# A two-phase MLP in an encoder kernel: all up blocks by seven Strassen products, the whole down product as one Strassen step

## What is computed

```python
h = rmsnorm(x, norm_mix_pre);  z = h @ w_in
a = rmsnorm(mla(...));  r = hgrn2(...)            # attention and a linear recurrence
x = x + rmsnorm(concat([a, r]) @ w_o, norm_mix_post)
h = rmsnorm(x, norm_mlp_pre)
m = square(relu(h @ w_up)) @ w_down               # 1024 x 1024 x 4096, then 1024 x 4096 x 1024
x = x + rmsnorm(m, norm_mlp_post)
e = p @ w_ple;  gate = sigmoid(x @ w_ple_gate)
x = x + rmsnorm(e * gate, norm_ple)
```

## Time and profile before

| | before |
|---|---|
| median of three runs | 1456.87 us |
| profiled execution, first to last instruction | 1456.6 us |
| PE busy (7132 matmuls) | 1434.9 us, 99% |
| DVE busy | 827.7 us, 57% |
| POOL busy | 706.1 us, 48% |
| ACT busy | 562.9 us, 39% |
| DMA, mean over the span | 80 GB/s |

### The profile page before, as it was taken

How to read it: one execution, slowest core, us unless ns; L and a number is a source line. 1 busy time by engine, 2 the same in 40 slices (tenths; PEclk the granted TensorE clock), 3 DMA queues, 4 the chain that set the end, 5 groups by cost and what they waited for, 6 DMA issues and landing times.

```text
span 1456.6 us, 19156 instructions
## 1 busy us (share of the span) xinstructions
PE 1434.9 (99%) x7132; PEld 1196.1 (82%) x7132; DVE 827.7 (57%) x1110; ACT 562.9 (39%) x1057; POOL 706.1 (48%) x562
## 2 busy tenths in 40 slices
PE   6999999999999999999999999999999999999998
PEld 5888888878749998888888888888888888888886
DVE  7135555444688885258774865545545554446475
ACT  6223232234247665345324333332222323344452
POOL 4284636265206424456565654455544444454481
PEclk9999999999999999999999999999999999999999
DMA  5221111102240004433533311111111114623252
GB/s 202 66 66 36 30 37 29 26 23 58 66 101 2 1 1 139 156 107 127 204 100 96 92 58 52 58 46 56 44 44 58 52 58 145 201 89 117 87 160 93
DMA packets 91725, 115.94 MB, mean 80 GB/s; under 512 B 13681, under 2 KB 54641, under 8 KB 91121
## 3 DMA queue, kind: packets, MB, share of 16 engines
q1 hardware_dynamic: 91632, 114.72, 25.7%
HBM read 102.11 MB, written 10.49 MB: 77 GB/s over the span
## 4 chain that ended last, share of the span: by engine, by line
PE 92%; DVE 4%; issue 2%; POOL 1%; ACT 1%; DMA 0%; SPq 0%; DVEq 0%; POOLq 0%; ACTq 0%
PE ps L50 25%; PE ps L52 25%; PE ps L51 25%; PE ps L922 4%; PE ps L1630 3%; PE ps L1637 2%; PE ps L1015 1%; PE ps L1439 1%; PE ps L969 1%; PE ps L954 1%; PE ps L966 0%; DVE total L2058 0%; PE ps L1010 0%; PE ps L1012 0%; DMA lb_raw<-in_hg_lb 0%
## 5 line engine op out<-in xcount | busy, mean ns | idle before, releaser
L1352 POOL TENSOR_TENSOR wy_low<-w_raw,wy_high 128x512 fp32r<-128x512 f32 x230 | 331.5, 1442 | 361.8 <-ACT wy_high L1333 361.6
L1333 ACT ACTIVATE wy_high<-w_raw 128x512 fp32r<-128x512 f32 x230 | 145.1, 631 | 391.9 <-PE ps L52 386.2
L50 PE MATMUL ps<-wy_high,hid_high 128*128 128x512 f32 x512 | 199.3, 389 | 0.4 <-DVE hid_low L1962 0.4
L52 PE MATMUL ps<-wy_high,hid_low 128*128 128x512 f32 x512 | 199.2, 389 | 0.0
L51 PE MATMUL ps<-wy_low,hid_high 128*128 128x512 f32 x512 | 199.2, 389 | 0.0
L2048 DVE TENSOR_TENSOR total<-total,ps 128x512 f32<-128x512 f32 x184 | 124.8, 687 | 101.3 <-PE ps L52 101.3
L370 POOL TENSOR_TENSOR wx_low<-w_raw,wx_high 128x512 fp32r<-128x512 f32 (+1 forms) x64 | 84.8, 1331 | 142.4 <-ACT wx_high L472 142.4
L50 PE MATMUL ps<-a_high,wy_high 128*128 128x512 f32 x352 | 137.5, 391 | 0.0
L52 PE MATMUL ps<-a_high,wy_low 128*128 128x512 f32 x352 | 137.0, 389 | 0.0
L51 PE MATMUL ps<-a_low,wy_high 128*128 128x512 f32 x352 | 137.0, 389 | 0.0
L50 PEld LDWEIGHTS ps<-wy_high,hid_high 128*128 128x128 f32 x512 | 96.1, 188 | 20.6 <-issue 0.6
(11 more groups left out here) (246 smaller groups left out, 3038.1 us busy)
## 6 DMA issues: line engine op xcount, KB each, us to landing
w_raw<-in_w_up SPq DMA_DIRECT2D x88, 256.0 KB, 2.8
w_raw<-in_w_down SPq DMA_DIRECT2D x88, 256.0 KB, 2.6
w_raw<-in_w_in SPq DMA_DIRECT2D x62, 256.0 KB, 2.8
w_raw<-in_w_o SPq DMA_DIRECT2D x32, 256.0 KB, 2.7
w_raw<-in_w_ple_gate SPq DMA_DIRECT2D x32, 256.0 KB, 2.6
x_tile<-in_x SPq DMA_DIRECT2D x8, 512.0 KB, 7.1
x_res<-in_x SPq DMA_DIRECT2D x8, 512.0 KB, 5.9
keep_x<-x_res SPq DMA_DIRECT2D x8, 512.0 KB, 3.9
```

The lines of the kernel that those rows point to most:

```text
L50: pe.matmul(out, stat_high, mov_high, start=start, stop=False)
L52: return pe.matmul(out, stat_low, mov_high, start=False, stop=stop)
L1333: act.activation(out, tile_raw(tile), ACT.Copy).then_inc(high_made, 1)
L1352: pool.tensor_tensor(low_tile, tile_raw(tile), high_tile.bitcast(F32), ALU.subtract).then_inc(low_made, 1)
```

## The change

The MLP becomes two phases. In the first, all sixteen blocks of 256 hidden columns are Strassen blocks. Two of the seven products of each block (`ep`) come first for all blocks, 32 tiles, because they need the tokens of the first half alone; the other five (`st`) follow, block by block, 80 tiles. The hidden layer isn't split any more when it is made: it is kept as float32 in four quarters (`hid11`, `hid12`, `hid21`, `hid22`), 26 of 64 tiles of it in DRAM (`keep_h`). In the second phase the whole down product is one Strassen step of seven products (`m`), each of 16 tiles; for each tile the sum of two hidden tiles, the sum or difference of two weight tiles, and the high and low part of each are made just before PE uses them. A tile of `ep`, `st` and `m` is 12 matmuls. The weight ring has six slots where it had four. In a block, DVE now makes the differences t1 and t3, and POOL t2 (of t1) and t4 (of t2). Some semaphores of the front are merged.

The diff, cut:

```diff
-            st_order = ["b11", "t2", "b21", "t3", "t1", "t4", "b22"]
+            BLOCKS, PAIRED, EP_COLS = 16, 8, 2 * P
+            st_order = ["t2", "t3", "t1", "t4", "b22"]
+            products = ["m4", "m7", "m1", "m3", "m2", "m5", "m6"]
+            quads = {"m4": ("21", "11"), "m7": ("21", "22"), "m1": ("11", "22"), "m3": ("12", "22"), "m2": ("11",),
+                     "m5": ("22",), "m6": ("11", "12")}
...
+            segs += [("ep", f, 0, 0) for f in range(PAIRED)]
+            segs += [("st", b, 0, 0) for b in range(BLOCKS)]
+            segs += [("m", j, 0, 0) for j in range(7)]
...
+            depth = {"wo": 8, "ep": 4, "st": 5, "m": 16, "gate": 8, "e": 2, "gr": 0}
...
-            RING, AHEAD = 4, 2
+            RING, AHEAD, APAIRS = 6, 2, 3
...
+                      tiles_of[EP_TILE + 6]: [(1, 4)], tiles_of[EP_TILE + 10]: [(1, 5)],
+                      tiles_of[EP_TILE + 12]: [(1, 6)], tiles_of[EP_TILE + 14]: [(1, 7)],
+                      (M6, 8): [(2, 0)], (M6, 10): [(2, 1)], (M6, 12): [(2, 2)], (M6, 14): [(2, 3)],
...
+            def pool_sums(n):
...
+                if kind == "st":
+                    return st_order[k] in ("t2", "t4")
+                return kind == "m" and products[segs[tiles_of[n][0]][1]] in ("m7", "m1", "m6") and k % 2 == 1
...
             def low(pool, n):
                 if n < TILES:
+                    if pool_sums(n + 1):
+                        weight_sum(pool, n + 1)
                     low_part(pool, ("pair", n))
+                    if n in difference_after:
+                        hidden_difference(pool, difference_after[n])
...
+            def weight_sum(pool, n):
...
+                if st_order[k] == "t2":
+                    raw_ready(pool, ("b22", b))
+                    pool.wait_ge(t_made, 2 * b + 1)
+                    one, two = raw_tile(("b22", b)), t_sum[1][:, :]
...
+            def op_high_of(act, n):
...
+                if n - M_TILE >= APAIRS:
+                    act.wait_ge(done, done_at["tile", n - APAIRS])
...
             def high(act, n):
                 if n < TILES:
                     high_of(act, ("pair", n))
...
+                if in_m(n):
+                    op_high_of(act, n)
...
+                        if n - base in ((3, 5), (4, 7))[h]:
+                            two = slice(4 * h + (n - base) // 5 * 2, 4 * h + (n - base) // 5 * 2 + 2)
                             roots_of(mean7x_made, two.start // 2 + 1, mean7x, rstd7x, rstd7x_made, two)
...
+                def first_sum(b):
+                    dve.wait_ge(p1_made, b + 1)
+                    dve.wait_ge(done, done_at["tile", EP_TILE + 4 * (b // 2) + 2 + b % 2])
...
+                    dve.tensor_tensor(first_tile(b)[:, :], p1_kept[:, b, :], ps[:, 2 + b % 2, :],
+                                      ALU.add).then_inc(first_added, 1)
...
                     tile7(o)
                     tile7(o + 1)
+                    if h:
+                        first_sum(0)
+                        first_sum(1)
...
+                first_sum(6)
+                first_sum(7)
+                s_chain(s1_raw, [(1, a21[0]), (1, a22[0]), (1, a21[1]), (1, a22[1])])
+                dve.wait_ge(s_step, s_steps[0])
+                s_chain(s2_raw, [(1, s1_raw), (-1, a11[0]), (-1, a11[1])])
+                first_sum(8)
+                first_sum(9)
+                dve.wait_ge(x_moved, 2 * 16 * TT)
+                s_chain(s3_raw, [(1, a11[0]), (-1, a21[0]), (1, a11[1]), (-1, a21[1])])
+                first_sum(10)
+                first_sum(11)
+                s_chain(s4_raw, [(1, a12[0]), (-1, s2_raw), (1, a12[1])])
+                s_low_of(1, s1_raw, 0)
+                s_low_of(3, s3_raw, 2)
+                first_sum(12)
+                first_sum(13)
+                s_low_of(2, s2_raw, 4)
+                s_low_of(4, s4_raw, 6)
+                weight_sums(0)
+                first_sum(14)
+                first_sum(15)
+                for b in range(BLOCKS):
...
+                    dve.wait_ge(done, late_done(b, 2))
+                    dve.wait_ge(u_made, 3 * b + 2)
...
+                    dve.tensor_tensor(comb1[:, :], u3[:, :], ps[:, late_bank(b, 2), :], ALU.add).then_inc(comb_made, 1)
+                    dve.tensor_tensor(u2[:, :], u2[:, :], ps[:, late_bank(b, 2), :], ALU.add).then_inc(u_made, 1)
+                    if b < BLOCKS - 1:
+                        weight_sums(b + 1)
+                    else:
+                        down_weight_sum(M_TILE)
+                    dve.wait_ge(done, late_done(b, 3))
...
+                    if b == BLOCKS - 1:
+                        down_weight_sum(M_TILE + 1)
+                        operand_low(M_TILE)
...
+                for n in range(M_TILE, M_TILE + MSTEPS):
+                    down_weight_sum(n + 3)
+                    operand_sum(n + 3)
+                    operand_low(n + 2)
+                    name, k = m_step(n)
...
+                    if behind == "m5":
+                        if k < 4:
+                            add_out("m5", k, "11")
+                            add_out("m5", k, "12")
...
+                        if k in (8, 9):
+                            add8(k - 8)
+                        if k in (11, 13):
+                            add8(2 + (k - 11) // 2)
...
+                def first_product(s, k, wh, wl):
+                    b, rows = 2 * segs[s][1] + k % 2, k // 2
+                    if b < 2:
+                        pe.wait_ge(a_split, 16 + 8)
+                    elif rows:
+                        pe.wait_ge(first_added, b - 1)
```

More of the change, by code:

```diff
@@ L1069, in banks_of @@
                     return [4 * n + i for i in range(4)]
[L1070 to L1075 removed]
+                if kind == "ep":
+                    return [0]
                 if kind == "st":
                     return [0]
+                if kind == "m":
+                    return [4 * ((f + 1) % 2) + i for i in range(4)]
                 if kind == "gate":
@@ L1166, in back_of @@
                         done_at["turn", a, b, part] = count
-                elif kind == "mm" and segs[a][0] == "st":
-                    count += 1
-                    done_at["prod", a, b] = done_at["tile", first[a] + b] = count
                 elif kind == "mm":
@@ L1323, in high_of @@
                 else:
-                    s, k = tiles_of[tile[1]]
-                    act.wait_ge(low_made, place["sum", st_order[k], segs[s][1]] + 1)
+                    sum_ready(act, tile[1])
                 if tile[0] == "res":
@@ L1990, in s_chain @@
-                            dve.tensor_tensor(out[here], left[here], part[here],
+                            dve.tensor_tensor(out[here], left[here], taken[here],
                                               ALU.add if sign > 0 else ALU.subtract).then_inc(s_step, 1)
@@ new lines, in down_weight_sum @@
+                def down_weight_sum(n):
+                    if n not in w_sum_at:
+                        return
+                    name, k = m_step(n)
+                    one, two = (("w" + quad, n) for quad in quads[name])
+                    raw_ready(dve, one)
+                    raw_ready(dve, two)
+                    if n == M_TILE + 1:
+                        dve.wait_ge(late_made, 2 * (3 * (BLOCKS - 1) + 1))
+                    elif sum_before(n) is not None:
+                        dve.wait_ge(low_made, place["pair", sum_before(n)] + 1)
+                    dve.tensor_tensor(sum_tile(n), raw_tile(one), raw_tile(two),
+                                      ALU.subtract if name in minus else ALU.add).then_inc(w_sum_made, 1)
@@ L2165, in dve_tail @@
+                dve.wait_ge(gains9_in, 32)
+                for i in range(4):
+                    add_out("m6", i, "22")
                 means8(1)
@@ L2254, in bank_free @@
+                    elif kind == "m" and f >= 2:
+                        out_read(pe, products[f - 2], i)
+                    elif kind == "m":
+                        bank = banks_of(s)[i]
+                        late_read(pe, *max((b, k) for b in (BLOCKS - 2, BLOCKS - 1) for k in range(5) if late_bank(b, k) == bank))
                     elif s == G00:
-                        pe.wait_ge(summed, sum_at[D10, i])
+                        pe.wait_ge(a_split, 32 + (6 if i < 2 else 8))
                     elif s == G01:
```

975 lines of the change are left out of this document (480 added, 495 removed).

## The result

The kernel after the change takes 1512.84 us (median of four runs, 1511.91 to 1513.88), the kernel before 1456.57 us beside it (four runs): a ratio of 1.0386, 95% interval 1.0371 to 1.0401. It is 3.9% slower, where 1.3% was forecast; the time lies above the range of 1452 to 1500. The profiled execution spans 1510.2 us.

The account below looks back on a forecast made before the run. PE was taken to bound the kernel: 264 fewer matmuls save 59.8 us of 1456.6, giving 1396.8. Adding 37 + 18 + 1 + 8 + 15 - 0.8 gave 1475 us, 1.3% slower; range 1452 to 1500.

Parts of the forecast that it names:

- the four places: Late blocks, early tiles, down product and turns inside m6, where engines' lists would make PE wait: 37, 18, 9, 15 us.
- Place 1: Late blocks: POOL's t2, waiting for DVE's t1, delays the fifth tile's low part; 2.48 us a block, 37 us.
- Place 2: Early tiles: DVE's chains, low parts and first_sums don't keep up with PE; 18 us of waits.
- rival of a covered block chain: Late blocks: the wait per block stays under 1.2 us, so the kernel gets faster; 1438 us with none; chance 0.10.
- full exclusion of DVE and POOL: Rival: DVE and POOL lock each other out, mainly costing the down product 11 us over forecast; 1494 us; chance 0.14.
- term for the granted clock: Whole kernel: PE taken at its upper clock, 2.4 GHz, throughout; nothing added to the sum for a fall.
- The clock falls in the new waits: Rival: waits of 5 us at tile 31 and in m6 bring 1.2 GHz; 5 to 10 us, 1483; chance 0.05.
- Place 3: Down product: 1 us for m4's first tile, 8 us for DVE and POOL slowing each other in m7 and m1.
- the 3.12 of the prediction: m7 and m1: DVE's and POOL's work makes a tile last 3.12 us, 0.4 too long.
- 5 us of lead: Down product: prepared parts are ahead of PE at the start; about 5 us taken off the cost of m7 and m1.
- low-load tiles: Down product: tiles in which the parts win back their lead over PE; no cost given.
- Place 4: Turns inside m6: add8 stands behind operand_low on DVE; PE waits 5.6 us, then three waits totalling 9.6; 15 us.

Follow-up runs that it names:

- edit 1: Changed kernel with DVE's two weight differences for the next block (t1, t3) moved up one tile, behind the second product's addition: 1460.53 us.
- edit 7: Changed kernel with POOL doing the low part of a block's fifth tile ahead of t2, blocks 0 to 14, DVE's list unchanged: 1473.3 us.
- edit 2: Changed kernel with ten extra matmuls on PE ahead of the wait for each block's fifth tile, blocks 0 to 14: 1503.4 us.
- edit 4: Changed kernel with all weight sums of m7, m1 and m6 on DVE, where POOL had every second one: 1503.75 us.
- edit 3: Changed kernel with the four turns inside m6 one tile later and add8 ahead of operand_low in DVE's list: 1491.59 us.
- edit 6: Changed kernel with edit 1, edit 3, edit 4 and edit 5 together: 1421.97 us, ratio 0.9757 to the kernel before.
- edit 9: Changed kernel with POOL making t2 of blocks 1 to 15 twice, to lengthen the wait at each block's fifth tile: 1550.36 us.
- edit 5: Changed kernel with first_sum of blocks 8 and 9 ahead of the second chain, and block 0's weight differences ahead of three low parts: 1509.65 us.
- edit 10: Changed kernel with DVE's t1 and t3 one addition earlier, between the two additions of the third product: 1491.74 us.

## Why the prediction was wrong

**Right:** the direction and the four places. PE has 6868 records. Place 1 was priced at 2.48 us a wait; by the starts of matmuls it is 2.5 (15 x 2.5 = 38, forecast 37), by the chain that was written down, and edits 1 and 7 take it away from either end. (In the list of waits it stands as 2.2, not as the 2.5 that the prediction expected there, because of the way idle time is counted.) Place 2, 18 forecast, 17.4 measured, is near for the wrong reason: 12.2 us are six waits, 1.8 their pauses, and 3.4 the lower clock, which the sum hadn't. Its own addends give 104 and 107 us where 103 and 106 were written, so 19 and not 18. The rival of a covered block chain fell: the wait is there each time. So did that of a full exclusion of DVE and POOL, below.

**The step that failed** is the term for the granted clock, which the sum has at nothing and the rival "The clock falls in the new waits" at 5 to 10 us with a chance of 0.05, by waits of 5 us alone ("2.5 each"). The runs show 15 stretches behind waits of 2.2 us and up, 107 slow matmuls, 21.4 us (23.8 with the slow turns), and edit 2 gives back 13.3 of them by keeping PE busy. The mechanism was named; its reach was wrong. It looked for a fall only behind the two longest kinds of wait, where the fifteen block waits of 2.2 us had nine stretches of 1.6 us, two thirds of the whole. And the rows against it were misread, twice, as PE's timeline of the kernel before and one window of it show:

```profile
7.91 1.94 PE L898 MATMUL ps<-ident,xn 128*128 128x128 f32 x8 [7.91 <-DVE xn L615]
...
16.50 0.63 PE L51 MATMUL ps<-wx_low,h_high 128*128 128x512 f32 x1
16.93 0.63 PE L52 MATMUL ps<-wx_high,h_low 128*128 128x512 f32 x1
...
333.43 4.87 PE L978 MATMUL ps<-ones,latent_sq 128*128 128x1 f32 x32
```

```profile
336.00:342.00 6.00, 6.00 (x28) 6.00 (x29) 1.65 (x3) 0.32 (x1) 2.78 (x3) 0.50 0.34 87
```

The clock column says 1.00 from 5 to 15 us, and so it does to 17 us. But eight turns at 7.91 us take 1.94 us, where eight at 22.08 take 1.04; and the two matmuls at 16.50 and 16.93 start 0.43 us apart with records of 0.63 us, as in the stretches at 0.50. So that column is no evidence of a clock that stayed up. Ahead of those turns PE had stood idle for 7.9 us, a gap of the kind that the prediction found in no row. And the clock was not at its upper level throughout: a digit 9 hides 6.8 us at 0.50 from 335.56 us on, which begin among 32 matmuls of a single column each.

The Trainium skill (TensorE: Matmul & The Clock Gate, "HAM oscillation") describes a kernel whose matmuls pause for each tile and then run at the lower clock, tile after tile, at a penalty of half the time spent there. By that rule, the trace agrees: 3.4 us at 0.50 for 1.6 us lost, nine times. The pauses that this section of the Trainium skill draws last 3 to 5 us; here waits of 2.2 us were enough in nine of fifteen cases, and the prediction was itself adding fifteen of them.

**Place 3 was mis-sized:** 9 us forecast. The windows of 20 us of the down product show where it went (an undisturbed one, as the third row, has 90 matmuls):

```profile
1113.00:1133.00 20.00, 18.34 (x75) 13.34 (x75) 19.90 (x17) 7.50 (x12) 15.43 (x11) 1.00 0.67 221
1133.00:1153.00 20.00, 18.75 (x78) 13.92 (x78) 19.96 (x20) 7.50 (x12) 15.27 (x10) 1.00 0.62 205
1193.00:1213.00 20.00, 20.00 (x90) 16.57 (x89) 14.27 (x16) 8.92 (x16) 9.62 (x8) 1.00 0.63 206
1273.00:1293.00 20.00, 18.72 (x79) 13.90 (x77) 20.00 (x19) 7.75 (x13) 16.77 (x11) 1.00 0.22 66
```

In m7 and m1 (first and second row) a tile lasts 12 x 20 / 77 = 3.1 us, the 3.12 of the prediction. The five windows from 1073 to 1173 are 56 matmuls short, 12.7 us; taken off were 5 us of lead that PE's parts should have had. The other part is in m2 and m5 (last row), costed at nothing as "low-load tiles" in which the lead is won back: POOL's hidden differences stand there, POOL is busy for 16.8 of 20 us, DVE for all 20, and the windows from 1233 to 1313 are 31 matmuls short, 7 us. So place 3 is about 20 us. Whole products say the same: m7 and m1 are 12.6 us over their 43.5, m2 and m5 6.9. That m2 and m5 are slowed by those differences is read from the windows and was not tried by an edit; edit 4 shows only that the weight sums on POOL are not what slows them.
For m7 and m1 the rule of the Trainium skill (SBUF — State Buffer, "SBUF: two separate sides") that DVE and POOL lock each other out fully would have given 3.46 us a tile. By that rule, the trace agrees only in that both get slower; the tile lasts 3.1. Place 3 as a whole did come to the 20 us that this rival would have it cost (19 and 1 for m4), but by chance: 12.6 in m7 and m1, where the rival has 24 before the lead is taken off, and 7 in m2 and m5, where it has nothing.

**Place 4 was mis-sized too:** 15 us forecast, 18.5 recorded (6.4 for the first where 5.6 was said, and 12.1 for three where 9.6 was), plus 1.2 for the pauses and 4.4 at the lower clock: 24, and edit 3 gave back 20. Three slow turns are 2.4 us more (1.62 in place of 0.79 to 0.85 each), and with a wait of 0.6 for `op_low` that makes up the 27.4 us that m6 is over its 47.2.

Put together: 1475 + 1 (place 1) + 13.6 (its clock) + 11 (place 3) + 5 (place 4) + 6.8 (its clock, slow turns included) - 3 (an earlier start and place 2) = 1509, the profiled 1510.2 but for 1 us.

**What stays open** is what decides between two waits of the same length: behind six of the fifteen waits of 2.2 us the clock stayed up, and in the kernel of edit 6 waits of 3.0 and 3.4 us left it at 1.00, while all of 3.6 us in edit 9 were followed by a fall. The table shows how often, not when. The traces hint that the moment of a wait counts beside its length. Edits 3, 4 and 5 keep the fifteen waits, and 9, 9 and 10 of them are followed by a slow stretch, but not in the same blocks. In the kernel after, the nine stretches begin 17.07 or 34.13 us apart, while the waits come 16.1 us apart (17.7 with a slow stretch between). And behind the 32 matmuls of one column in the front the clock falls in ten of the twelve traces, but not in those of the kernel after and of edit 10. No run was made to test this.

## What to carry to other kernels

In a kernel bound by TensorE, price a new wait at more than its length: here a pause cost 0.3 us beyond its recorded idle time, and one of 2.2 us another 1.6 us in nine of fifteen cases, at the lower clock. When work is spread over engines by lists, look at which operation an urgent one stands behind: moving two of DVE's operations up by one tile, or letting POOL do the urgent low part first, was worth 52 and 40 us of 1513. And give a loaded DVE more rather than leave POOL working beside it, if the trace shows that its operations shrink when POOL stops (1.77 to 0.68 us here) by more than the operation itself takes on DVE (0.6). Last, a clock column at 1.00 is to be held against the distance between matmuls before it is used as evidence.

## What was not expected of the hardware

In the late blocks the clock's answer is steep in the length of the pause: a fall behind none of fifteen waits of 1.6 us, nine of fifteen at 2.2 us, fifteen of fifteen at 3.6 us. But length isn't all, since single waits of 3.0 and 3.4 us left it up. It also fell in the front with no pause in PE's records, among matmuls of a single column. Filling a pause with ten useless matmuls made the kernel 9 us faster (1512.8 to 1503.4). And where DVE and POOL meet in m1, DVE pays 2.6 times its time (0.68 to 1.77 us), POOL 1.2 times (1.29 to 1.52). That is not a fixed ratio: in edit 5, where DVE's operations are as long as POOL's, the two pay alike (1.2 to 2.1 and 1.27 to 2.25 us).
